# Second attention's probabilities turned by VectorE and on-chip DMAs; the order of an FFN's moves and of the second layer's loads changed

## The reference, cut to what matters

```python
h = x + 0.5 * swiglu(rmsnorm(x), ffn1)            # w_gate, w_up [2048, 5504], w_down [5504, 2048]
proj = rmsnorm(h) @ w_in                          # q, k, v, u
h = h + concat(rmsnorm(s5_mixer(u)), rmsnorm(dilated_attention(q, k, v))) @ w_out
h = h + 0.5 * swiglu(rmsnorm(h), ffn2)
x = rmsnorm(h, final_norm)                        # end of the first block
# second block: one trunk layer, with a context sequence ctx of 256 tokens
m = silu(c) @ w_mod + b_mod                       # shift, scale and gate, for x and for ctx
p = modulated(layer_norm(x)) @ w_in_2             # mLSTM inputs, q, k, v of an attention, gates
h_a = mlstm(...)                                  # seeded by the state of ctx
def attend_blocks(q, k_all, v_all):               # 16 heads of 128, 4 key/value heads, 512 keys
    s = einsum(q, k_all) * 128 ** -0.5            # [128 queries, 512 keys], twice per head
    p = softmax(s)                                # exp(s - max) / sum
    return einsum(p, v_all)
out = layer_norm(alpha * x + gate * (branch_merge(h_a, o_attn, ...) @ w_out_2))
```

## Time and profile before

| | us |
|---|---|
| median of 3 runs (3177.61 to 3181.41) | 3180.91 |
| the profiled execution's own time | 3181.68 |
| its span, first to last instruction | 3179.9 |
| TensorE busy | 3147.3 (99%) |
| VectorE busy | 2104.6 (66%) |
| ScalarE busy | 1478.6 (46%) |
| POOL busy | 492.8 (15%) |

### The profile page before, as it was taken

How to read it: one execution, slowest core, us unless ns; L and a number is a source line. 1 busy time by engine, 2 the same in 40 slices (tenths; PEclk the granted TensorE clock), 3 DMA queues, 4 the chain that set the end, 5 groups by cost and what they waited for, 6 DMA issues and landing times.

```text
span 3179.9 us, 41806 instructions
## 1 busy us (share of the span) xinstructions
PE 3147.3 (99%) x15148; PEld 2595.7 (82%) x15148; DVE 2104.6 (66%) x2530; ACT 1478.6 (46%) x1835; POOL 492.8 (15%) x743
## 2 busy tenths in 40 slices
PE   9999999999999999999999999999999999999998
PEld 8888888888778888888878878888878877888886
DVE  6888875556986678888866554665666755445556
ACT  5444444445346444444444435544454554544443
POOL 1111108948650001111100000000000100000000
PEclk9999999999999999999999999999999999999999
DMA  8999986556453689999976655546866643665664
GB/s 260 295 307 307 301 263 219 187 189 195 133 160 112 197 248 310 302 297 299 288 230 210 196 185 175 169 150 180 161 145 192 187 131 100 182 196 179 212 185 152
DMA packets 411102, 666.67 MB, mean 210 GB/s; under 512 B 114568, under 2 KB 123024, under 8 KB 410304
## 3 DMA queue, kind: packets, MB, share of 16 engines
q1 hardware_dynamic: 384176, 567.21, 56.8%
q0 software_dynamic: 26768, 97.35, 11.7%
HBM read 647.93 MB, written 2.10 MB: 204 GB/s over the span
## 4 chain that ended last, share of the span: by engine, by line
PE 95%; DVE 2%; DMA 1%; ACT 1%; issue 1%; SPq 0%; POOL 0%; ACTq 0%; DVEq 0%; POOLq 0%
PE acc L301 24%; PE acc L303 24%; PE acc L302 24%; PE pst L1030 2%; PE pst L1032 2%; PE pst L1031 2%; PE acc L1030 2%; PE acc L1032 2%; PE acc L1031 2%; PE pst L2779 1%; PE pst L2761 1%; PE pst L2471 1%; DVE w_lo L249 1%; DMA w_raw<-in_ffn_w_up 1%; PE pst L2473 0%
## 5 line engine op out<-in xcount | busy, mean ns | idle before, releaser
L249 DVE TENSOR_TENSOR w_lo<-w_raw,w_hi 128x1024 fp32r<-128x1024 f32 x1059 | 1314.4, 1247 | 889.4 <-ACT w_hi L242 881.9
L242 ACT ACTIVATE w_hi<-w_raw 128x1024 fp32r<-128x1024 f32 x1059 | 1122.0, 1061 | 1418.4 <-PE acc L303 1028.7
L301 PE MATMUL acc<-w_hi,act_hi 128*128 128x512 f32 (+1 forms) x3360 | 1320.4, 393 | 3.3 <-DVE w_lo L249 2.7
L303 PE MATMUL acc<-w_hi,act_lo 128*128 128x512 f32 (+1 forms) x3360 | 1302.3, 388 | 0.0
L302 PE MATMUL acc<-w_lo,act_hi 128*128 128x512 f32 (+1 forms) x3360 | 1300.9, 387 | 0.0
L301 PEld LDWEIGHTS acc<-w_hi,act_hi 128*128 128x128 f32 x3360 | 631.1, 188 | 132.7 <-issue 5.5
L303 PEld LDWEIGHTS acc<-w_hi,act_lo 128*128 128x128 f32 x3360 | 630.7, 188 | 128.0
L302 PEld LDWEIGHTS acc<-w_lo,act_hi 128*128 128x128 f32 x3360 | 631.5, 188 | 122.9 <-issue 0.5
L723 POOL DMA_DIRECT2D mod_ring<-in_w_mod x160 | 115.9, 725 | 914.4 <-DVE pst L739 753.3
L739 DVE SCALAR_TENSOR_TENSOR pst<-mod_ring,c_act,pst 128x512 f32<-128x512 f32 x300 | 226.0, 753 | 17.0 <-DMA mod_ring<-in_w_mod 11.1
L1030 PE MATMUL acc<-w_hi,g_hi 128*128 128x512 f32 x344 | 136.2, 396 | 5.9 <-DVE w_lo L249 3.3
(11 more groups left out here) (468 smaller groups left out, 2399.1 us busy)
## 6 DMA issues: line engine op xcount, KB each, us to landing
w_raw<-in_w_in SPq DMA_DIRECT2D x400, 512.0 KB, 3.7
w_raw<-in_ffn_w_down SPq DMA_DIRECT2D x168, 512.0 KB, 3.9
w_raw<-in_ffn_w_gate SPq DMA_DIRECT2D x160, 512.0 KB, 5.3
w_raw<-in_ffn_w_up SPq DMA_DIRECT2D x160, 512.0 KB, 6.8
mod_ring<-in_w_mod POOLq DMA_DIRECT2D x160, 512.0 KB, 6.2
w_raw<-in_w_out SPq DMA_DIRECT2D x64, 512.0 KB, 3.8
w_raw<-in_w_branch_a SPq DMA_DIRECT2D x32, 512.0 KB, 4.0
w_raw<-in_w_branch_b SPq DMA_DIRECT2D x32, 512.0 KB, 4.6
```

The costliest lines, as they stand in the source:

```text
L242: act.activation(weight_tiles(s)[0], w_raw[:, s % SLOTS, :], ACT.Copy).then_inc(w_hi_done, 1)
L249: dve.tensor_tensor(lo, w_raw[:, s % SLOTS, :], hi.bitcast(F32), ALU.subtract).then_inc(w_lo_done, 1)
L301: pe.matmul(o, xh, wh, start=k == 0, stop=False)
L303: mm = pe.matmul(o, xl, wh, start=False, stop=k == 2 * nch - 1)
```

## The change

The second attention. Score banks are three instead of two. ScalarE exponentiates in place in PSUM. VectorE turns the 128x512 probabilities in 32x32 blocks into `a2_blocks` (two buffers, one per head). When both halves of a head are turned, SP and POOL each issue 8 DMAs of 32 partitions, which carry the blocks to `a2_keys`, also double. TensorE multiplies these by the values five steps behind the scores (`A2_LAG`), and VectorE normalises six behind. The steps are 38. SP's moves for a head stand behind one load, counted in x_ga's chunks and on into x_zb's. TensorE's turns and ScalarE's copy are gone.

```diff
-        ATT2_STEPS = NQ + 4
+        A2_LAG = 5
+        ATT2_STEPS = NQ + A2_LAG + 1
+        A2_MOVED = 16 * 8
         def attention2_step_pe(pe, s):
             if s < NQ:
-                if s >= 2:
-                    pe.wait_ge(a2_probs, s - 1)
+                if s >= 3:
+                    pe.wait_ge(a2_turned, s - 2)
                 head, h = s // 2, s % 2
-                pe.matmul(pst[:, s % 2, :], qb_t[...], keys_t[...], ...).then_inc(a2_scores, 1)
+                pe.matmul(pst[:, s % 3, :], qb_t[...], keys_t[...], ...).then_inc(a2_scores, 1)
-            u = s - 2
-                (waits, then four pe.transpose(pst[:, 2, ...], probs2[...], ident[:]), then_inc a2_turned)
-            u = s - 3
+            u = s - A2_LAG
             if 0 <= u < NQ:
+                for queue in range(2):
+                    pe.wait_ge(a2_moved[queue][head % 2], A2_MOVED * (head // 2 + 1))
                 if u >= 1:
                     pe.wait_ge(a2_fetched, u)
                 for b in range(4):
-                    mm = pe.matmul(pst[:, 3, 0:HD_B], probs2_t[:, u % 2, b * P:(b + 1) * P], ...)
+                    mm = pe.matmul(pst[:, 3, 0:HD_B], a2_keys[head % 2][:, 4 * h + b, :], ...)
         def attention2_step_dve(dve, s):
+            u = s - 1
+            if 0 <= u < NQ:
+                head, h = u // 2, u % 2
+                dve.wait_ge(a2_probs, u + 1)
+                for queue in range(2) if head >= 2 else ():
+                    dve.wait_ge(a2_moved[queue][head % 2], A2_MOVED * (head // 2))
+                dve.transpose(a2_blocks[:, head % 2, :, h, :, :]..., pst[:, u % 3, :]...).then_inc(a2_turned, 1)
-            u = s - 4
+            u = s - A2_LAG - 1
             (reciprocal, scaling into ob, then_inc a2_fetched; then the maximum of s, as before)
+        def attention2_move(eng, head, queue):
+            eng.wait_ge(a2_turned, 2 * head + 2)
+            if head >= 2:
+                eng.wait_ge(a2_out, 2 * head - 2)
+            for g in (2 * queue, 2 * queue + 1):
+                for d in range(4):
+                    eng.dma_start(a2_keys[head % 2][32 * d:32 * d + 32, :, 32 * g:32 * g + 32],
+                                  a2_blocks[32 * g:32 * g + 32, head % 2, d, :, :, :].rearrange("p h b c -> p (h b) c")
+                                  ).then_inc(a2_moved[queue][head % 2], 16)
+        def attention2_move_sp(sp, n):
+            for head in range(NH_B):
+                if -(-(2 * head + 3) * 32 // ATT2_STEPS) - 1 + 8 == n:
+                    attention2_move(sp, head, 0)
```

The FFNs (both). In the last block one move instead of two goes behind each up load; the other eight go behind the first four down loads. ScalarE's `hi_tiles` of block NB-2 moves behind the rounding of s+17, VectorE's `lo_tiles` behind the split of s+19:

```diff
-                        if m and not first(b):
-                            move_gated_sp(sp, n_use, b - 1, j)
+                        if m and last(b):
+                            move_gated_sp(sp, n_use, b - 1, (j,))
+                        elif m and not first(b):
+                            move_gated_sp(sp, n_use, b - 1, (2 * j, 2 * j + 1))
...
-                    if q == 0 and 8 <= j < 16:
-                        move_gated_sp(sp, n_use, NB - 1, j - 8)
+                    if q == 0 and j < 4:
+                        move_gated_sp(sp, n_use, NB - 2, (8 + 2 * j, 9 + 2 * j))
+                    elif q == 0 and 8 <= j < 16:
+                        move_gated_sp(sp, n_use, NB - 1, (2 * j - 16, 2 * j - 15))
...
-                split_ahead(act, s, 16, i, 16, 8 + LEAD, 12 + LEAD)
+                hi_at = 14 if last(b) else 12
+                split_ahead(act, s, 16, i, 16, 8 + LEAD, hi_at + LEAD)
                 if not first(b):
                     hi_tiles(act, n_use, b - 1)
...
-                        if j == 13:
+                        if j == (15 if last(b) else 13):
                             lo_tiles(dve, n_use, b - 1)
```

The second layer's loads. POOL issues all mod loads ahead of ctx_nat, and the first half's statistics move later:

```diff
-        CX_STATS = ((0, 16), (1, 22))
-        CX_ROOT = ((0, 18), (1, 24))
-        CX_NORM = ((0, 20), (1, 25))
+        CX_STATS = ((0, 21), (1, 22))
+        CX_ROOT = ((0, 23), (1, 24))
+        CX_NORM = ((0, 25), (1, 25))
...
-            mod_loads_pool(pool, 8 * MOD_PASSES["ffn2"], 8 * N_MODS - 4)
+            mod_loads_pool(pool, 8 * MOD_PASSES["ffn2"], 8 * N_MODS)
...
-                if h == 0:
-                    mod_loads_pool(pool, 8 * N_MODS - 4, 8 * N_MODS)
```

More of the change, by code:

```diff
@@ L782, in first, with last @@
             return isinstance(b, int) and b == 0
+        def last(b):
+            return isinstance(b, int) and b == NB - 1
         def width(b):
@@ L828, in turn_gated_dve, with move_gated_sp @@
                           pst[:, 0:2, 0:n].rearrange("p h (t c) -> p h t c", c=P)).then_inc(g_turned, 1)
-        def move_gated_sp(sp, n_use, b, j):
-            if j == 0:
+        def move_gated_sp(sp, n_use, b, pairs):
+            if 0 in pairs:
                 sp.wait_ge(g_turned, b + (NB * n_use + 1))
             n = width(b) // P
-            for pair in range(2 * j, 2 * j + 2):
+            for pair in pairs:
                 src, dst = pair // GROUPS, pair % GROUPS
@@ L865, in it @@
                 ins.then_inc(fetched[0], 1)
-                split_ahead(act, s, 16, i, 16, 8 + LEAD, 12 + LEAD)
+                hi_at = 14 if last(b) else 12
+                split_ahead(act, s, 16, i, 16, 8 + LEAD, hi_at + LEAD)
                 if not first(b):
                     hi_tiles(act, n_use, b - 1)
-                split_ahead(act, s, 16, i, 16, 12 + LEAD, 16 + LEAD)
+                split_ahead(act, s, 16, i, 16, hi_at + LEAD, 16 + LEAD)
                 if n_use == 0 and first(b):
@@ L1105, in pairs, with stream_sp @@
                     body(i, s0, i * (2 * nch) + s0, i + p0)
-        def stream_sp(sp, name, w, col0, first_k=0):
+        def stream_sp(sp, name, w, col0, first_k=0, behind=None):
             nch = job(name)[2]
@@ L1114, in body @@
                                    c + nch * m + j)
-            pairs(sp, name, body, unrolled=bool(first_k))
+                        if behind is not None:
+                            behind(sp, nch * (2 * i + m) + j)
+            pairs(sp, name, body, unrolled=bool(first_k) or behind is not None)
         def stream_pe(pe, name, between=None, turning=None, halves=False, operand=None, flip=0, first_k=0):
@@ L1981, in build @@
         assert r.o <= top2
-        probs2 = at("probs2", [P, 2, BLK], offset=area5)
-        probs2_t = at("probs2_t", [P, 2, BLK], offset=area5 + 4 * 2 * NKV_B * HD_B)
+        a2_blocks = at("a2_blocks", [P, 2, 4, 2, 4, 32], offset=area5)
+        a2_keys = [at(f"a2_keys{n}", [P, 2 * 4, P], offset=o) for n, o in enumerate((-(-r.o // 64) * 64, top2))]
+        assert -(-r.o // 64) * 64 + 4096 <= top2
         ob_hi = at("ob_hi", [P, KT, SEQ], F32R, offset=area3)
@@ L2010, in build @@
             sem("a2_" + n) for n in ("scores", "max", "probs", "turned", "out", "fetched"))
-        a2_copied = sem("a2_copied")
+        a2_moved = [[sem(f"a2_moved_{q}{n}") for n in range(2)] for q in ("sp", "pool")]
         gr_turned, gr_copied, gr_spread = sem("gr_turned"), sem("gr_copied"), sem("gr_spread")
@@ L2757, in attention2_step_pe @@
             if s < NQ:
-                if s >= 2:
-                    pe.wait_ge(a2_probs, s - 1)
+                if s >= 3:
+                    pe.wait_ge(a2_turned, s - 2)
                 head, h = s // 2, s % 2
-                pe.matmul(pst[:, s % 2, :], qb_t[:, head, h * P:(h + 1) * P], keys_t[:, head // 4, :],
+                pe.matmul(pst[:, s % 3, :], qb_t[:, head, h * P:(h + 1) * P], keys_t[:, head // 4, :],
                           start=True, stop=True).then_inc(a2_scores, 1)
-            u = s - 2
+            u = s - A2_LAG
             if 0 <= u < NQ:
[L2765 to L2770, removed]
-            u = s - 3
-            if 0 <= u < NQ:
-                head = u // 2
-                pe.wait_ge(a2_copied, u + 1)
+                head, h = u // 2, u % 2
+                for queue in range(2):
+                    pe.wait_ge(a2_moved[queue][head % 2], A2_MOVED * (head // 2 + 1))
                 if u >= 1:
@@ L2778, in attention2_step_pe @@
                 for b in range(4):
-                    mm = pe.matmul(pst[:, 3, 0:HD_B], probs2_t[:, u % 2, b * P:(b + 1) * P],
+                    mm = pe.matmul(pst[:, 3, 0:HD_B], a2_keys[head % 2][:, 4 * h + b, :],
                                    vals[:, b, kv * HD_B:(kv + 1) * HD_B], start=b == 0, stop=b == 3)
@@ L2786, in attention2_step_act, with attention2_step_dve @@
                 act.wait_ge(a2_max, u + 1)
-                if u >= 2:
-                    act.wait_ge(a2_turned, u - 1)
-                act.activation(probs2[:, u % 2, :], pst[:, u % 2, :], ACT.Exp, scale=SCALE_B,
+                act.activation(pst[:, u % 3, :], pst[:, u % 3, :], ACT.Exp, scale=SCALE_B,
                                bias=row2[:, 0, u:u + 1], accum_out=row2[:, 1, u:u + 1]).then_inc(a2_probs, 1)
-            u = s - 2
+        def attention2_step_dve(dve, s):
+            u = s - 1
             if 0 <= u < NQ:
[L2793 to L2798, removed]
-            u = s - 4
+                head, h = u // 2, u % 2
```

(15 more changed lines are left out.)

## The result

The changed kernel took 3196.01 us (median of 5 runs, 3190.53 to 3197.01), the kernel before on the same chip 3180.01: ratio 1.0045, 95% interval 1.0032 to 1.0059. It is slower by 14 to 16 us. The forecast was 3183.0, "no change"; the time lies just inside its range of 3170 to 3197, and outside the band of 0.2%, up to 3187.3, that the prediction called no change.

The account below looks back on a forecast made before the run. TensorE, busy 99% of the span, was taken as the bound. Terms -14.1 + 8.3 + 2.6 + 6.0 + 4.5 - 5.2 = +2.1 us on 3181.7 gave 3183.8, or 3183.0 on the median's scale; range 3170 to 3197.

Parts of the forecast that it names:

- Turns: Second attention: taking four turns per step off TensorE saves 0.44 us in each of 32 steps, -14.1 us.
- Pair waits: Second attention: in paired steps TensorE's values wait 1.65 us for VectorE's normalisation, five times, +8.3 us.
- Rival C: Second attention: the 1.65 us waits also dip the clock, giving 3191.5 us; chance 0.1.
- Late moves: Second attention: SP's last move lands 1.4 us late at heads 11 and 14 only, taken as +2.6 us.
- Rival B: Second attention: the moves become what x_ga waits for, giving 3195 us; chance 0.18.
- FFN1's hand-over: FFN1's last block: down starts 4.7 us after up's end, +4.3, plus a clock dip of 1.7: +6.0 us.
- FFN2's, +4.5: FFN2's last block: the late last move makes down start near 1572.9 instead of 1568.4, +4.5 us.
- The low clock behind the wait: At the FFNs' down starts: TensorE's wait is followed by a lower granted clock, costing 1.7 us.
- FFN2's up wait of 2.24: FFN2's last block: fewer moves among the up loads should remove TensorE's 2.24 us wait for a split.
- Order of mod loads: Second layer, mod loads before ctx_nat: removes TensorE's 3.5 us wait and a 1.7 us clock dip, -5.2 us.
- Rival D: Order of mod loads: no help, as ctx_nat or the statistics hold VectorE instead, giving 3188 us; chance 0.07.

Follow-up runs that it names:

- e6: Kernel before without TensorE's four turns and ScalarE's copy in the second attention, values reading unturned probabilities (computation left out): 3165.75 us, ratio 0.9954.
- e5: The second attention's change alone on the kernel before, with VectorE normalising first and turning behind it: 3175.71 us, ratio 0.9984.
- e9: e8 with SP's moves of every head placed one load sooner: 3160.98 us, ratio 0.9934 to the kernel before.
- e2: Kernel before with only the second layer's new order of mod loads and ctx_nat, and the later statistics: 3177.06 us, ratio 0.9987.
- e7: Kernel before with only hi_tiles and lo_tiles of block NB-2 two chunks later, all moves where they were: 3192.05 us, ratio 1.0040.
- e3: Kernel before with only the second attention's change: 3181.47 us, ratio 0.9999.
- e4: Changed kernel with down_pe's wait for block NB-2's g_lo moved to before chunk 18 of the first down quarter: 3177.81 us, 0.9989 to the kernel before.
- e8: Changed kernel with FFN moves and tiles put back, e4's later wait and e5's VectorE order: 3165.54 us, ratio 0.9951 to the kernel before.
- e10: Kernel before with only the new order of mod loads and e4's later wait: 3172.01 us, ratio 0.9968.
- e11: The changed kernel run again unchanged, also called the repeat: 3195.53 us, ratio 1.0041 to the kernel before.

## Why the prediction held in its steps and its range, and fell short in its sum

Every mechanism of the forecast is in the trace, but three terms were too small: the two hand-overs and the waits for ob. By its own band of 0.2% the kernel is slower, by 0.41 to 0.45%, where the prediction gave no change 0.43 and slower 0.35.

**Turns, -14.1: right.** e6 gives -14.2. The other bound was misread: 19.2 us is not what the group's records add up to (128 of 272 ns are 34.8), but the busy time, in which records that overlap one another count once.

**Pair waits, +8.3: right in kind, short by one cause.** Five waits in pairs, released by the scaling into ob. The chain from the pair's first score was put at 4.25 us and measured 4.08 (2619.81 to 2623.89); the waits are 1.47 instead of 1.65, 7.4 in all. e5 shows the cause, since they go when the order on VectorE is turned round. Rival C did not occur: none of these waits dipped the clock. Overlooked was a wait that I had not priced at all, VectorE's for the reuse of a2_blocks: two more waits for ob, +2.5.

**Late moves, +2.6 at heads 11 and 14: the sum held by luck.** Head 11 was on time. Head 14 was 2.38 late (3.01 in the repeat), not 1.4, and that from two errors. Its values come in step 33, and steps 32 and 33 have no score product; the count gave each of them 0.86 us, so TensorE was ready at 2714.71, T+11.4 with T at 2703.29, and not at T+13.3. SP's last move started at 2714.52, T+11.2 as forecast, and landed within 2.6 us instead of 3.5. The median landing was 3.4 against 3.5 from the earlier trace rows; the estimate of 2.1 us worked out from the Trainium skill (DMA: Bandwidth & Descriptors, "Anatomy of one DMA", a section on DMAs that GpSimd issues: a fixed cost near 2 us and the rest by bytes) is near only the fastest, 1.8, and POOL's moves taken alone have the same median of 3.4. By it the move would have landed at 2716.6, and head 14 would have been 1.9 late, not on time as the prediction has it. Rival B's mechanism, moves that TensorE waits for, was there but at one head of 16, so it is not what made the kernel slower; that the time came out beside its 3195 is chance. e9 shows how near to the edge the moves stood: a place one load sooner on SP takes them off the path.

**FFN1's hand-over, +6.0: measured +8.4. FFN2's, +4.5: measured +8.3.** These are the failed terms, 6.2 of the 8.3 us between the sum and the profiled difference. What failed is the time at which the last move lands. The page counts landing from the start of a move's own issue, and so do these numbers. In FFN1 I had the last move issued 4.7 us before up ends and landed 3.8 later, 0.9 before the end; it was issued at 477.55, 4.4 before, and landed 5.0 later, 0.6 after the end. From the landing to the start of down I had 5.6 us (4.7 + 0.9) and it took 5.6 (482.55 to 488.13): the chain of roundings and splits was right to a tenth. In FFN2 all lies 9.2 us later than in the kernel before, so my 1563.0 for up's end is 1572.2, as measured; my issue near 1561.4 is 1570.6 and was 1571.68; my landing at 1566.4 is 1575.6, and was 1578.86, so the move took 7.2 us and not 5. The chain behind it took 7.0 against 6.5. For FFN1 I had taken landing from rows where the moves share the DMAs with up loads alone; the DMA share there, 456 to 476 us of the kernel before, is 0.86. The last moves now share them with down loads and, in FFN2, with a mod load: the share is 1.01 from 477.5 to 482.5 and 1.08 from 1571.7 to 1578.9. The page's overall median for just this move, 5.8 us, was in my own table and lies between the two, 5.0 and 7.2; I used it only for rival B. In the kernel before, the moves of FFN2's last block (1538 to 1556 us) already took 5.5 in the median and up to 7.1.
The low clock behind the wait, 1.7, was right in FFN2 and 0.8 short in FFN1, where it lasted 5.4 us into the down product.

**FFN2's up wait of 2.24: right.** 0.2 is left, and up ends where forecast.

**Order of mod loads, -5.2: right.** -5.4 in the changed kernel, -5.3 in e2's trace and 4.7 by its medians. Rival D did not occur.

**The range** held the time by 1 us, because its upper end reached past rival B, which is not what happened. Both hand-overs passed their upper bounds, +8 (8.4) and +7 (8.3): these had no room for moves that take 5.0 and 7.2 us to land.

What stays open: why the clock fell behind a wait of 2.38 us before and not behind 2.22 at head 14; and why x_kv and x_o show a dip in one execution and not in the next. The +0.8 to +1.2 us at the very start, where nothing was changed, are no effect of the change: the other profiled executions, whose start is the same too, lie from 0.0 (e7) to +1.2 (e3). It goes mostly with when the granted clock first rose: at 6.1 us before and 6.3 in e7, at 8.8 and 8.7 in the changed kernel and its repeat.

## What to carry to other kernels

When work is moved to behind a stage's last loads, follow the one wait that the next stage makes on it, back to the DMA, and price that landing with the queues that it will then have beside it, at both ends: the slow end decided here. Put the consumer's wait at the first instruction that uses the data; a wait at the head of a stage turns a harmless delay into an idle TensorE, and the same holds for an engine in between (ScalarE here) that stops in program order for late data. Where two producers share an engine in order, as the turn and the normalisation on VectorE, run first the one for which the bound engine waits.

## What the runs showed of the hardware that was not expected

- The granted clock falls during an idle stretch already, not only once TensorE resumes: in FFN2 it was 0.50 over all of 1576.0 to 1585.8 us, with TensorE empty. The dip was 13.7 us long (from 1575.5), the one in FFN1 6.8 (from 486.7), those of the kernel before, up to 3100 us, 3.4 each. Only what lies behind the resumption costs: 3.4 us at 0.51 and some 5.4 near 0.5.
- Waits of some 2 us can go either way. One wait of 2.02 us in x_o (2338.20 to 2340.22 in the kernel before) stands in all 13 profiled executions; in 6 of them (before, e2, e4, e8, e10, e11) 3.4 us at 1.2 GHz followed, in 7 none. Of the others between 100 and 3100 us, waits of 2.16 and 2.38 had a dip and waits of 2.03, 2.22, 2.24, 2.49 and 2.55 had none; every one of 3.01 us or more had one, and none of those from 1.3 to 1.7.
- The clock also fell without a wait: behind sixteen 8x8 matmuls at the start of x_kv, 2208.0 to 2209.9 us of the changed kernel (low from 2210.4). It did so in 6 of the 13 profiled executions (the changed kernel, e2, e8, e9, e10, e11); in the kernel before, the same matmuls had no dip.
- The 32 KB moves with 128-byte runs landed in a median of 2.4 us in e9 and 3.5 in e8, the same DMAs placed one weight load apart (min 1.9 and 1.8, max 4.6 and 5.1).
- Issue of such a move took 0.61 us on SP and 0.585 on POOL; POOL's was priced at 0.72 from mod_ring's loads, so a head's eight were 1.1 us quicker than forecast.
